# Reordering the GLA stage of a hybrid decoder step, and moving its key-value scaling from VectorE to ScalarE

## What is computed

```python
def step(state, inp):                       # one chunk of 128 tokens
    qc, kc, vc, gc = inp
    bc = jnp.cumsum(gc, axis=2)
    ...
    o = (jnp.einsum('bhts,bhsv->bhtv', scores, vc)
         + jnp.einsum('bhtd,bhdv->bhtv', qc * jnp.exp(bc), state))
    k_dec = kc * jnp.exp(b_last - bc)
    state = (jnp.exp(b_last[:, :, 0, :])[..., None] * state
             + jnp.einsum('bhsd,bhsv->bhdv', k_dec, vc))
```

## Time and profile before

| | |
|---|---|
| timed runs | 1786.56, 1782.37, 1785.96 us; median 1785.96 |
| the profiled execution | 1782.07 us, its span 1780.3 us |
| mean granted clock of PE | 0.981 of full speed |
| busy, share of span | PE 96%, PEld 88%, DVE 46%, POOL 42%, ACT 22% |

### The profile page before, as it was taken

The page is one execution under the profiler, slowest core; times in us unless marked ns, Lnnn a source line. Parts: engine busy times, 40 slices in busy tenths (PEclk is TensorE's granted clock), DMA queues, the critical chain, the costliest instruction groups (busy, mean ns, idle before and its releaser), DMA issues.

```text
span 1780.3 us, 29377 instructions
## 1 busy us (share of the span) xinstructions
PE 1713.2 (96%) x11760; PEld 1565.8 (88%) x11760; DVE 825.0 (46%) x1318; ACT 395.2 (22%) x704; POOL 750.1 (42%) x584
## 2 busy tenths in 40 slices
PE   7999999998999889999999999999999999999995
PEld 7967677776877879999999999999999999999994
DVE  4156767641335272111165658525434533542527
ACT  4133233321323231011120552110110011011133
POOL 4310111101112023333345546976686686686325
PEclk9899999998998989999999999999999999999998
DMA  5244445404651031111112121211111121121202
GB/s 160 62 115 133 127 122 143 121 13 116 191 154 29 9 88 47 47 47 47 47 36 83 52 78 32 71 48 42 54 57 39 49 66 31 48 66 42 89 25 95
DMA packets 176009, 130.24 MB, mean 73 GB/s; under 512 B 22394, under 2 KB 148762, under 8 KB 175762
## 3 DMA queue, kind: packets, MB, share of 16 engines
q1 hardware_dynamic: 170258, 127.24, 24.7%
q10 hardware_dynamic: 5632, 1.35, 0.5%
HBM read 117.63 MB, written 10.92 MB: 72 GB/s over the span
## 4 chain that ended last, share of the span: by engine, by line
PE 83%; DVE 9%; issue 2%; ACT 2%; DMA 2%; SPq 1%; POOL 0%; DVEq 0%; ACTq 0%; POOLq 0%
PE psum L1601 7%; PE psum L1606 6%; PE psum L1605 6%; PE psum L994 5%; PE psum L997 5%; PE psum L998 5%; PE psum L1666 4%; PE psum L1055 4%; PE psum L1668 4%; PE psum L1059 4%; PE psum L1667 4%; PE psum L1061 4%; PE psum L1210 3%; PE psum L1503 3%; PE psum L1507 3%; PE psum L1506 2%
## 5 line engine op out<-in xcount | busy, mean ns | idle before, releaser
L858 POOL CAST wh<-raw 128x1024 fp32r<-128x1024 f32 x72 | 86.4, 1200 | 788.2 <-PE psum L1055 386.9
L860 POOL TENSOR_TENSOR wl<-raw,wh 128x1024 fp32r<-128x1024 f32 x72 | 190.3, 2642 | 5.8
L887 POOL TENSOR_TENSOR wl<-raw,wh 128x512 fp32r<-128x512 f32 x126 | 168.9, 1341 | 10.1
L1055 PE MATMUL psum<-xh,wh 128*128 128x352 f32 (+1 forms) x480 | 161.6, 337 | 1.5 <-DVE ql L2362 1.5
L1601 PE MATMUL psum<-xh,wh 128*128 128x258 f32 x576 | 162.5, 282 | 0.0
L1605 PE MATMUL psum<-xl,wh 128*128 128x258 f32 x576 | 162.4, 282 | 0.0
L1606 PE MATMUL psum<-xh,wl 128*128 128x258 f32 x576 | 162.2, 282 | 0.0
L994 PE MATMUL psum<-xh,wh 128*128 128x344 f32 (+1 forms) x480 | 157.4, 328 | 4.7 <-POOL wl L860 3.3
L1059 PE MATMUL psum<-xl,wh 128*128 128x352 f32 (+1 forms) x480 | 160.1, 334 | 0.0
L1061 PE MATMUL psum<-xh,wl 128*128 128x352 f32 (+1 forms) x480 | 159.1, 331 | 0.0
L997 PE MATMUL psum<-xl,wh 128*128 128x344 f32 (+1 forms) x480 | 155.9, 325 | 0.0
(11 more groups left out here) (388 smaller groups left out, 4250.0 us busy)
## 6 DMA issues: line engine op xcount, KB each, us to landing
raw<-in_w_in SPq DMA_DIRECT2D x86, 256.0 KB, 3.3
parts<-in_cache_k SPq DMA_DIRECT2D x64, 256.0 KB, 3.0
parts<-in_cache_v SPq DMA_DIRECT2D x64, 256.0 KB, 3.0
raw<-in_w_gate SPq DMA_DIRECT2D x44, 256.0 KB, 3.0
raw<-in_w_up SPq DMA_DIRECT2D x44, 256.0 KB, 2.9
raw<-in_w_down SPq DMA_DIRECT2D x44, 256.0 KB, 2.8
raw<-in_w_o SPq DMA_DIRECT2D x28, 256.0 KB, 3.0
cb<-negc_scratch SPq DMA_DIRECT2D x8, 520.0 KB, 5.4
```

The costliest lines, as they stand in the source:

```text
L1055: ins = mm(out, wt(wh, slot, k), xh[:, k, c0:c0 + cw], start=(k == 0), stop=False)
```

## The change

In the front the turn of v0 moves behind v1, which goes through a second buffer `gvT1`. For pair 1 the first q chunk is computed in pair 0's tail, ahead of the square sums; the logits come chunk by chunk, the third behind two chunks of k; both value panels are computed before any turn, in banks of their own. The first chunk of the first merge panel is computed in pair 1's tail. SP issues the first merge panels before `values_spread(1)`, and POOL splits panels 28 and 30 at other events. In the chunk loops ACT scales the key-value product, with Identity and a scale per partition, and DVE only waits for it.

```diff
@@ SP
-            values_spread(1)
...
-            with sp.Fori(0, KT) as m:
+            merge_panels(0)
+            values_spread(1)
+            with sp.Fori(1, KT) as m:
                 merge_panels(m)
@@ POOL split
-                if last is not None:
+                if isinstance(p, int) and p == PAN_MERGE:
+                    pool.wait_ge(sem("panel_used"), p - 1)
+                if isinstance(p, int) and p == PAN_MERGE + 2:
+                    pool.wait_ge(sem("vs_ready"), 3)
+                elif last is not None:
                     pool.wait_ge(sem("panel_used"), last + 1)
@@ PE front
-            turn((gvT,), FRONT["vt0"], [(gvT,)])
             whole(G0 + 3, 0, "v1")
             sample_outputs(7)
             whole(G0 + 3, 1, "v1")
             whole(G0 + 3, 2, "v1")
+            turn((gvT,), FRONT["vt0"], [(gvT,)])
             for b in FRONT["v1"]:
                 settled(b)
-            turn((gvT,), FRONT["vt1"], [(gvT,)])
+            turn((gvT1,), FRONT["vt1"], [(gvT1,)])
@@ PE pair 1 (part_job is one chunk of job, logit_chunk one of gate_logits)
-                    job(p, slot_of(p), A3, ALL8, X8)
-                    gate_logits(1, G_LG)
-                    job(p + 1, slot_of(p + 1), B3, ALL8, X8)
-                    job(p + 2, slot_of(p + 2), A3, ALL8, X8)
+                    part_job(p, slot_of(p), A3[1], 1)
+                    part_job(p, slot_of(p), A3[2], 2)
+                    logit_chunk(1, 0, G_LG[0])
+                    logit_chunk(1, 1, G_LG[1])
+                    part_job(p + 1, slot_of(p + 1), B3[0], 0)
+                    part_job(p + 1, slot_of(p + 1), B3[1], 1)
+                    logit_chunk(1, 2, G_LG[2])
+                    part_job(p + 1, slot_of(p + 1), B3[2], 2)
+                    for v in range(2):
+                        for c in range(3):
+                            part_job(p + 2 + v, slot_of(p + 2 + v), G_V[v][c], c)
                     for b in B3:
                         settled(b)
                     turn((ke,), G_KTURN, [])
-                    job(p + 3, slot_of(p + 3), B3, ALL8, X8)
-                    for b in A3:
+                    for b in G_V[0]:
                         settled(b)
                     turn((gvT,), G_VTURN[0], [(gvT,)])
-                    for b in B3:
+                    for b in G_V[1]:
                         settled(b)
-                    turn((gvT,), G_VTURN[1], [(gvT,)])
-                for b in range(8):
+                    turn((gvT1,), G_VTURN[1], [(gvT1,)])
+                for b in range(6):
                     settled(b)
@@ PE tail (G_V = [[6, 7, 0], [1, 2, 3]], SQ_BANKS = [(6, 7), (3, 4), (5, 4)])
-                for q in (0, 2, 4, 5):
+                for q in (0, 2):
+                    settled(q)
+                p = PAN_GLA + GH + 4 if i == 0 else PAN_MERGE
+                part_job(p, slot_of(p), A3[0], 0, CHUNKS if i == 0 else BODY)
+                for q in (4, 5):
                     settled(q)
                 square_sums(0)
...
+            for c in (1, 2):
+                part_job(PAN_MERGE, 1, A3[c], c, BODY)
+            merge_rest(PAN_MERGE)
@@ ACT chunk loop
-                        skip([2 * (c % 2), 6 + c % 2])
+                        skip([2 * (c % 2)])
+                        kvb = 6 + c % 2
+                        filled(kvb)
+                        if c > 0:
+                            act.wait_ge(sem("state_ready"), NT * i + c)
+                        for h in range(2):
+                            rows = slice(64 * h, 64 * h + 64)
+                            ins = do(kvs[rows, :], psum[rows, kvb, h * P:(h + 1) * P], ACT.Identity,
+                                     scale=gl[rows, 1, c:c + 1])
...
@@ DVE chunk loop
-                    filled(6 + par)
-                    for h in range(2):
-                        rows = slice(64 * h, 64 * h + 64)
-                        ins = ve.tensor_scalar(kvs[rows, :], psum[rows, 6 + par, h * P:(h + 1) * P],
-                                               gl[rows, 1, c:c + 1], None, ALU.mult)
...
+                    skip([6 + par])
+                    if c > 0:
+                        dve.wait_ge(sem("stp_ready"), 8 * i + c)
                     settled(6 + par)
                     dve.wait_ge(sem("kvs_half"), NT * i + c + 1)
```

More of the change, by code:

```diff
@@ L260 @@
 G_OS = 6
+G_V = [[6, 7, 0], [1, 2, 3]]
+SQ_BANKS = [(6, 7), (3, 4), (5, 4)]
 A3, B3 = [0, 1, 2], [3, 4, 5]
@@ L421, in build @@
         gvT = nc.alloc_sbuf_tensor_at("gvT", [P, T], F32, offset=OHB + HALF + 2 * size([P, T], F32))
+        gvT1 = nc.alloc_sbuf_tensor_at("gvT1", [P, T], F32, offset=OHB + HALF + 3 * size([P, T], F32))
         gl, eg, vs_tok = c("gl", [P, 3, NT]), c("eg", [P, NB]), b("vs_tok", [NB, 2 * P])
@@ L861, in split @@
                     .then_inc(sem("panel_split"), 1)
-            for p in range(27):
+            LATE = PAN_MERGE + 5
+            for p in range(LATE):
                 split(slot_of(p), raw_use(p), p, last_in(slot_of, p))
-            with pool.Fori(27 // RING, PANELS // RING) as i:
+            with pool.Fori(LATE // RING, PANELS // RING) as i:
                 for s in range(RING):
-                    split(s, i + raw_use(27 + s) - 27 // RING, RING * i + s, RING * i + s - RING)
+                    split(s, i + raw_use(LATE + s) - LATE // RING, RING * i + s, RING * i + s - RING)
             steps = [14]
@@ L1376, in _, with part_job, logit_chunk @@
             whole(G0 + 3, 2, "v1")
+            turn((gvT,), FRONT["vt0"], [(gvT,)])
             for b in FRONT["v1"]:
                 settled(b)
-            turn((gvT,), FRONT["vt1"], [(gvT,)])
+            turn((gvT1,), FRONT["vt1"], [(gvT1,)])
             pe.wait_ge(sem("po_ready"), NB)
+            def part_job(p, slot, bank_, c, chunks=CHUNKS):
+                pe.wait_ge(sem("panel_split"), p + 1)
+                take(bank_)
+                c0, cw = chunks[c]
+                out = psum[:, bank_, 0:cw]
+                for k in range(KT):
+                    first = mm(out, wt(wh, slot, k), xh[:, k, c0:c0 + cw], start=(k == 0), stop=False)
+                    if c == 0 and k == 0:
+                        first.then_inc(sem("panel_used"), 1)
+                    mm(out, wt(wh, slot, k), xl[:, k, c0:c0 + cw], start=False, stop=False)
+                    last = mm(out, wt(wl, slot, k), xh[:, k, c0:c0 + cw], start=False, stop=(k == KT - 1))
+                give(bank_, last)
+            def logit_chunk(i, c, b):
+                c0, cw = CHUNKS[c]
+                pe.wait_ge(sem("alr_loaded"), 16 * i + 16)
+                take(b)
+                last = mm(psum[:, b, 0:cw], wa2[:, i * P:(i + 1) * P], alrT[:, c0:c0 + cw], start=True, stop=True)
+                give(b, last)
             for i in range(2):
@@ L1460, in _, with merge_rest @@
                 square_sums(2)
-            with pe.Fori(0, KT - 1) as m:
-                B.loop(m, [2, 2, 2, 2, 2, 2, 0, 0])
-                p = PAN_MERGE + 3 * m
-                job(p, 1, A3, ALL8, X8, chunks=BODY)
+            def merge_rest(p):
                 job(p + 1, 2, B3, ALL8, X8, chunks=BODY)
@@ L1470, in _ @@
                 job(None, 0, B3, [4, 5, 6, 7], ((oh, ol), [4, 5, 6, 7]), release=False, chunks=BODY)
-                B.end(KT - 1)
+            for c in (1, 2):
+                part_job(PAN_MERGE, 1, A3[c], c, BODY)
+            merge_rest(PAN_MERGE)
+            with pe.Fori(0, KT - 2) as m:
+                B.loop(m, [2, 2, 2, 2, 2, 2, 0, 0])
+                p = PAN_MERGE + 3 + 3 * m
+                job(p, 1, A3, ALL8, X8, chunks=BODY)
+                merge_rest(p)
+                B.end(KT - 2)
             def part_of_merge(slot, b, c, ks, x, releases):
@@ L1985, in values_turned, with values_copied @@
                     read(b, ins)
-            def values_copied(banks):
+            def values_copied(banks, to):
                 for c, (c0, cw) in enumerate(CHUNKS):
                     filled(banks[c])
-                    read(banks[c], do(gvT[:, c0:c0 + cw], psum[:, banks[c], 0:cw], ACT.Copy))
+                    read(banks[c], do(to[:, c0:c0 + cw], psum[:, banks[c], 0:cw], ACT.Copy))
             act.wait_ge(sem("scores_read"), 2 * len(PIECES) * 4)
@@ L2065, in _ @@
                 for h in range(2):
-                    for b in (A3, B3)[h]:
-                        settled(b)
+                    for c in range(3):
+                        settled(SQ_BANKS[c][h])
                     do(gsq[:, h, :], gsq[:, h, :], ACT.Exp, scale=-0.5).then_inc(sem("root_ready"), 1)
@@ L2678, in _ @@
                 skip([4 + (NT - 1) % 2])
-                skip([G_OS] + A3 + B3)
+                skip([G_OS] + [b for pair in SQ_BANKS for b in pair])
                 dve.wait_ge(sem("go_ready"), 10 * i + 10)
```

24 lines of the change are left out of this document (12 added, 12 removed).

## The result

The changed kernel takes 1766.45 us (median of four runs, 1765.84 to 1766.95), the kernel before beside it 1786.26: a ratio of 0.989, 95% interval 0.9875 to 0.9906. The forecast was 1771, with a range of 1763 to 1780. The profiled execution took 1766.5 us around a span of 1764.8. First the busy time by engine, from its page (before: the earlier trace rows).

The account below looks back on a forecast made before the run. VectorE was taken to bound the loop at 2.09 us a chunk, TensorE close behind at 1.94. Six terms summed to 12.4 us: 1769.7 against the profiled execution, 1773.6 against the median; forecast 1771, range 1763 to 1780.

Parts of the forecast that it names:

- b: Loop of pair 0: with the scalings on ScalarE, TensorE becomes the bound at 1.94 us a chunk; gain 1.7 us.
- the rival of ACT's queue: Chunk loops: ScalarE's scaling queues behind its copy and square, a 3.9 us ring; slower, 1800.7 us, chance 0.04.
- e: Loop of pair 1: splits leave it, scalings move, low clock at its start kept; gain 5.3 us (3.2 to 7.8).
- a: Front: turn of v0 moves behind v1 into the wait there, with a second buffer; gain 0.8 us (0 to 1.6).
- d: Pair 1's projections, second q chunk to first key-value product: gain 1.5 us (0 to 3.2) despite a 3.1 us stall.
- c: Tail of pair 0: first q chunk ahead of the square sums; gain 3.1 us (0.5 to 4.8).
- f: Tail of pair 1 and merge: first merge chunk moves ahead, but a chain stands behind; gain 0 (-0.3 to 2.5).
- the clock stays up: Rival: chunks put into the tails hold the clock; 18.3 us gained in all, 1763.8 us, chance 0.20.
- The clock falls oftener: Rival: two turns in a row ahead of pair 0's loop lower the clock; 7.3 us gained, 1774.8 us, chance 0.13.

Follow-up runs that it names:

- e1: The changed kernel with VectorE scaling the key-value products again, so the reordering alone: 1773.34 us, ratio 0.9946 to the kernel before.
- e12: The changed kernel with pair 1's two turned values sharing one buffer again: 1772.97 us, ratio 0.9934 to the kernel before.
- e5: The changed kernel with pair 1's first q chunk back behind pair 0's last square sums: 1770.38 us, ratio 0.9922 to the kernel before.
- e6: The changed kernel with the first merge chunk back behind pair 1's last square sums: 1771.07 us, ratio 0.9923 to the kernel before.
- e7: The changed kernel with the front's turn of v0 ahead of v1 again, second buffer kept: 1772.52 us, ratio 0.993 to the kernel before.

## Why the prediction was right, and where its steps were off

**b held.** DVE led, PE leads now, 1.94 a chunk; 1.8 measured, 1.7 forecast. ACT's scaling took 0.75 a pair, the bound of 0.76, and the rival of ACT's queue never showed: with two chunks in flight it costs PE nothing. The reordering alone puts 1.7 a loop on the scaling, from both sides.

**e was the step mis-sized most: 5.3 forecast, 8.0 measured.** The part that failed is "plus the low clock at the loop's start, which I keep", priced at 2.5. I had noted in a that a second buffer lets both turns stand together, and did not carry it to pair 1, where the earlier trace rows shows the wait of 1.74 for the one buffer. With one buffer back the fall comes back and the loop takes 3.0 more; this is shown. The rest is right in sum: of the 5.3, 1.7 were the scalings and 3.6 the splits; of the 8.0, the scalings are 1.7 (e1), the loop's start 3.0 (e12), and 3.3 are left for the splits. The run with the splits in the loop shows what such a loss is made of, two fifths stall and three fifths clock, and that it is the state's scalings that meet the subtraction.

**d: 1.5 forecast, 1.0 measured.** The stall of 3.1 came as 2.96, on DVE's decayed q, ahead of the third v chunk. The fall behind it, 1.7, did not come in this profile; it comes in half of them. PE came back 33.5 us after the second q chunk's start, not 32.1, 0.7 of it the tail's fall that reaches in here, and the turns took 6.9 from the last product (607.0), not 6.0. So 1.7 one way and 2.2 the other: errors of opposite sign, and by the count above the fall that stayed away is luck.

**c: 3.1 forecast, 4.2 measured.** The 4.8 at full clock set a tail that had lost 5.1 us to the clock against one that had not; the work was nearly the same. The moved chunk alone is worth some 0.6 (e5); the rest is that falls of before did not come, and why they did not is not shown. The 1.7 for the fall behind the tail came as I let it, 1.0 here and 0.7 in d.

**a: 0.8 forecast, 1.3 measured**, inside its ends. The turn's place gives 0.6, and the second buffer by difference 0.7. **f: 0 forecast, 0.6 measured.** The third panel starts 0.29 behind the product before it, where products follow 0.16 apart: PE waits 0.1 for the chain, so both end together, and the run without the chunk shows no work won or lost.

**Sum and rivals.** 12.4 forecast, 17 measured in the six stretches, less 2.2 in the untouched front. That loss (3.4 us more of low clock, 1.2 less of the rest) belongs to these two profiles, since in all 14 the low clock costs the front between 13.6 and 18.8, and it brings the sum nearer to the forecast than the terms are: luck, so far. The means of all runs stand 17.5 apart. The time lies between the forecast (1769.7) and *the clock stays up* (1763.8): that rival came true for e, for d in this profile, and not for the tails. What spoke against it, that all three falls of the earlier trace rows follow thin work which stays, was wrong for the largest: the wait ahead of it did not stay. *The clock falls oftener* is not the changed kernel (0.985 against 0.980), but three of its variants (e5, e6, e7) sit at 0.982 to 0.983, 4 to 6 us slower with full-clock times within half a microsecond.

Left open: what decides whether the clock falls behind the 2.96 us wait and at the end of a loop, and why edits that leave such a place untouched (e6 and e7 in d's stretch) change how often it does, or whether that is the chip. No run here varies that alone.

## What to carry to other kernels

Before a low clock is carried over into the sum, look for the wait that stands right ahead of it, and ask whether the change removes that wait; here one second buffer was worth 0.8 us of waiting and 3 us of clock behind it. Compare variants by time multiplied by granted clock beside time, since a few falls outweigh the edits. Keep thin work in one piece (spread between dense products it cost 8 us here), and put the producers that a long chain waits for (here a logit chunk) ahead of dense work that nobody waits for yet.

## What was not expected of the hardware

- ACT's Identity with a scale, 64x128 out of PSUM, took 0.75 us for two: as long each as its copy of 128x256 (0.38), so half the columns on half the partitions saved nothing, and it was no faster than DVE's two scalings (0.72).
- In these stretches lost clock came in pieces of 1.7 us, one or two in a row, at the tails, behind some waits and at some loop ends; only under the mixed tails did it last (6.8 and 5.1).
- A busy PE did not protect the clock: windows with PE busy for 4.00 of 4.00 us stood at 0.50 when single-column products were among the dense ones.
